# Expert loop: gather indices placed apart from the scatter's, sample's down products first and in another bank; attention: maxima moved ahead of a subtraction, one split step later

## What is computed

```python
def attend(q_blk):                       # 8 heads, query/key width 96, value width 64
    s = jnp.einsum('bqhd,bkhd->bhqk', q_blk, k)
    p = jax.nn.softmax(s, axis=-1)
    return jnp.einsum('bhqk,bkhd->bqhd', p, v)

def ec_moe(x, w_router, w_gate, w_up, w_down):     # 16 experts choose their tokens
    cap = max(1, EC_CAPACITY * N // N_EXPERTS)     # 256 of the prompt, 32 of the sample
    aff = jax.nn.softmax((xt @ w_router).astype(jnp.float32), axis=-1)
    gates, idx = lax.top_k(aff.T, cap)
    xs = xt[idx]
    h = jax.nn.silu(einsum(xs, w_gate)) * einsum(xs, w_up)     # 1024 -> 512
    y = einsum(h, w_down) * gates[..., None]                   # 512 -> 1024
    out = jnp.zeros((N, D), x.dtype).at[idx.reshape(-1)].add(y.reshape(-1, D))
```

## Time and profile before

| | us |
|---|---|
| median of 3 runs (lowest, highest) | 3238.51 (3237.43, 3239.25) |
| the profiled execution, its own time | 3233.96 |
| its span in the profile | 3232.1 |
| PE busy in the span | 2797.7 (87%) |
| DVE, ACT, POOL busy | 1780.7, 1564.5, 1089.2 |

### The profile page before, as it was taken

The page is one execution under the profiler, slowest core; times in us unless marked ns, Lnnn a source line. Parts: engine busy times, 40 slices in busy tenths (PEclk is TensorE's granted clock), DMA queues, the critical chain, the costliest instruction groups (busy, mean ns, idle before and its releaser), DMA issues. The chain is left out here.

```text
span 3232.1 us, 42082 instructions
## 1 busy us (share of the span) xinstructions
PE 2797.7 (87%) x15335; PEld 1523.0 (47%) x15335; DVE 1780.7 (55%) x2604; ACT 1564.5 (48%) x2488; POOL 1089.2 (34%) x969
## 2 busy tenths in 40 slices
PE   7999999959999999968976896999910899999998
PEld 4555555525555555522322232444400665566655
DVE  3344444448888888755567553333279444544443
ACT  3333333329999999955426441222240444444440
POOL 1111111127888888852036100121120232332321
PEclk9999999969999999989988997999955999999999
DMA  5112222224211111058975896443340556566562
GB/s 149 47 54 80 63 81 82 75 76 164 93 34 34 34 34 34 8 211 331 302 247 228 309 317 204 128 130 117 96 176 0 169 179 204 182 206 211 179 190 41
DMA packets 246139, 444.32 MB, mean 137 GB/s; under 512 B 55022, under 2 KB 136046, under 8 KB 244272
## 3 DMA queue, kind: packets, MB, share of 16 engines
q1 hardware_dynamic: 188608, 355.42, 33.1%
q0 software_dynamic: 10752, 37.75, 5.3%
q10 hardware_dynamic: 46608, 48.92, 4.7%
HBM read 290.25 MB, written 151.73 MB: 137 GB/s over the span
## 5 line engine op out<-in xcount | busy, mean ns | idle before, releaser
L959 POOL TENSOR_TENSOR at_p<-at_pf,at_p 128x512 f16<-128x512 f32 x424 | 515.3, 1227 | 143.8 <-ACT at_p L1093 119.9
L1221 DVE TENSOR_REDUCE at_mxs<-at_pM 128x1 f32<-128x512 f32 x512 | 342.3, 684 | 83.3 <-PE at_pM L1120 74.7
L578 PE MATMUL pj_ps<-pj_xT,pj_wch 128*128 128x512 f32 (+1 forms) x960 | 381.0, 550 | 0.8 <-issue 0.8
L1092 ACT ACTIVATE at_pf<-at_pS,at_scale 128x512 f32<-128x512 f32 x520 | 358.3, 689 | 40.5 <-PE at_pS L1145 40.4
L1093 ACT ACTIVATE at_p<-at_pS,at_scale 128x512 f16<-128x512 f32 x520 | 355.3, 683 | 0.0
L1164 PEld LDWEIGHTS at_pO<-at_vv,at_p 128*128 128x128 f16 x4160 | 234.0, 97 | 143.8 <-POOL at_p L959 34.6
L1164 PE MATMUL at_pO<-at_vv,at_p 128*128 128x129 f16 x4160 | 268.0, 207 | 10.2 <-POOL at_p L959 8.3
L578 PEld LDWEIGHTS pj_ps<-pj_xT,pj_wch 128*128 128x128 f32 x960 | 179.2, 190 | 167.9 <-issue 162.6
L1973 PE MATMUL mg_pU<-z,mg_yT 128*128 128x512 f32 x576 | 252.9, 597 | 0.2 <-ACT mg_yT L1882 0.2
L2540 PE MATMUL ex_pY<-mo_down,ex_hT 128*128 128x512 f32 x512 | 222.5, 592 | 0.7 <-issue 0.7
L1120 PE MATMUL at_pM<-at_k,at_q 96*128 96x512 f16 x512 | 190.1, 390 | 29.9 <-DVE at_q L1207 16.1
(11 more groups left out here) (279 smaller groups left out, 5360.4 us busy)
## 6 DMA issues: line engine op xcount, KB each, us to landing
sp_rows<-s_F SPq DMA_DIRECT2D x76, 768.0 KB, 6.9
s_F<-fs_a SPq DMA_DIRECT2D x72, 768.0 KB, 4.8
mo_raw<-in_w_gate SPq DMA_DIRECT2D x32, 1024.0 KB, 9.6
mo_raw<-in_w_up SPq DMA_DIRECT2D x32, 1024.0 KB, 10.1
mo_down<-in_w_down SPq DMA_DIRECT2D x16, 2048.0 KB, 11.1
s_G<-sp_gg ACTq DMA_DIRECT2D x72, 256.0 KB, 6.2
sp_tab<-tab_spec SPq DMA_DIRECT2D x76, 192.0 KB, 4.4
s_QK<-pj_R ACTq DMA_DIRECT2D x18, 768.0 KB, 4.4
```

The costliest lines, as they stand in the source:

```text
L578: last = pe.matmul(pU[n % 2][:, 0:width], wch[ch % 2][:, k, :], xT[:, k, t0:t0 + width], start=(k == 0), stop=(k == KD - 1))
L959: eng.tensor_tensor(p2[r][:, :], pf[:, r, :], p1[r][:, :], ALU.subtract).then_inc(own_done if n in own else others_done, 1)
L1092: act.activation(pf[:, n % 4, :], pS[n % 2][:, 0:QB], ACT.Exp, scale=scale[:, 0:1])
L1221: dve.tensor_reduce(mxs[:, j // NC, j % NC:j % NC + 1], pM[j % 2][:, :], AX.X, ALU.max).then_inc(pM_free, 1)
```

## The change

In the experts, `place` is cut in two. `place_gather(e + 1)` copies the gather's indices alone, at the start of the step, with no wait, and signals a semaphore of its own, `listed_g`, on which the gather now waits. `place(e)` copies the scatter's indices and the gates of the expert in hand, after `leave_x(e + 1)`, behind the wait for the scatters of expert e - 2. The order of the down products, their evictions and scatters is now sample, prompt tile 0, prompt tile 1 (DOWN_ORDER). The sample's products go into pU[1], one bank wide, in four groups of partitions, and not into pY; PE waits for its evictions before the next expert's second up product writes pU[1].

In attention, at the steps with a `move` (n % 16 = 7) DVE issues the `move` first and `rest` after it; at all other steps the order is as before. The twelfth split piece of heads 1 on is made at step 38, not 33 (it is the low part of one quarter of q, L1210).

```diff
--- before.py
+++ after.py
@@ -867,7 +867,7 @@
-    split_at = [1, 9, 11, 12, 14, 15, 17, 25, 27, 28, 30, 33, 41, 43, 44, 46]
+    split_at = [1, 9, 11, 12, 14, 15, 17, 25, 27, 28, 30, 38, 41, 43, 44, 46]
     first_split_at = [3, 6, 9, 11, 12]
     second_split_at = [22, 25, 27, 28, 30, 31, 33, 41, 43, 44, 46, 47, 49, 50, 52, 57]
     v_split_at = [5 + 14 * m for m in range(V_SPLITS)]
@@ -1275,11 +1275,16 @@
             def head(h, b):
                 for n in range(NS):
-                    rest_ahead(dve, own, h, n)
-                    for m in leads_in(h, n):
-                        ahead = leading(h, b, m)
+                    blocks = [leading(h, b, m) for m in leads_in(h, n)]
+                    moved = any(ahead and ahead[3] == last_in(ahead[0]) for ahead in blocks)
+                    if not moved:
+                        rest_ahead(dve, own, h, n)
+                    for ahead in blocks:
                         if ahead:
                             lead(*ahead)
+                    if moved:
+                        rest_ahead(dve, own, h, n)
                     if n % KT in range(norm_at, norm_at + 3):
                         part = (n % KT - norm_at,)
                         if n >= KT:
@@ -2058,6 +2063,8 @@
 PARTS = P // CAPS[1]
+DOWN_ORDER = (2, 0, 1)
 W_PARTS = 4
@@ -2380,7 +2387,7 @@
         part = sb("part", [CAPS[1], 512])
         wts, ticks = sem("wts"), sem("ticks")
         d_in = weights["d_in"]
-        placed = sem("placed")
+        listed_g, placed = sem("listed_g"), sem("placed")
         gathered = [sem(f"gathered{b}") for b in range(2)]
         x_low, multiplied, backed = sem("x_low"), sem("multiplied"), sem("backed")
         x_turned, xT_ready, gate_made, up_made = sem("x_turned"), sem("xT_ready"), sem("gate_made"), sem("up_made")
@@ -2432,7 +2439,7 @@
                 pool.tensor_tensor(mark[:, 1:2], mark[:, 0:1], mark[:, 0:1], ALU.add).then_inc(ticks, 1)
             def gather(e, b):
-                pool.wait_ge(placed, 3 * e + 3)
+                pool.wait_ge(listed_g, e + 1)
                 if not early(e):
                     pool.wait_ge(x_turned, TURNS * (e - 1))
                 tick((NC + 1) * e - NC if not isinstance(e, int) or e else 0)
@@ -2447,9 +2454,10 @@
                     gather(e + 1, 1 - b)
                 if not (isinstance(e, int) and e == 0):
                     pool.wait_ge(scattered, 16 * NC * e)
-                for c, (g, _, n) in enumerate(SLOT_TILES):
-                    pool.wait_ge(y_ready, 2 * NC * e + 2 * c + 2)
-                    tick((NC + 1) * e + 1 + min(more, 1) + c)
+                for i, c in enumerate(DOWN_ORDER):
+                    g, _, n = SLOT_TILES[c]
+                    pool.wait_ge(y_ready, 2 * NC * e + 2 * i + 2)
+                    tick((NC + 1) * e + 1 + min(more, 1) + i)
                     out = io[("y_prompt", "y_sample")[g]][0]
                     pool.indirect_dma_start(out=out, out_offset=bass.IndirectOffsetOnAxis(ap=now_s[b][0:n, c:c + 1], axis=0),
                                             in_=ys[b][c][0:n, :], in_offset=None, compute_op=ALU.add).then_inc(scattered, 16)
@@ -2521,6 +2529,8 @@
                     for g, (out, done, free) in enumerate(((pG, gate_made, silued), (pU, up_made, h_ready))):
                         if not (isinstance(e, int) and e == 0 and f < 2):
                             pe.wait_ge(free, FT * e + f - 1)
+                        if f == 1 and g and not (isinstance(e, int) and e == 0):
+                            pe.wait_ge(y_ready, 2 * NC * (e - 1) + 2)
                         if f == 0:
                             pe.wait_ge(weights["lo_made"], W_PARTS * e + 2 * g + 2)
                         for k in range(KD):
@@ -2532,25 +2542,26 @@
                     turn(e + 1, 1 - b)
                 pe.wait_ge(d_in[b], 8 * e - 8 * b + 16)
                 pe.wait_ge(h_ready, FT * e + FT)
+                at, n = starts[2], CAPS[1]
+                for r in range(2):
+                    for j in range(4):
+                        f, h = 2 * (j // 2) + r, j % 2
+                        last = pe.matmul(pU[1][n * j:n * j + n, :], hT[:, f, at:at + n],
+                                         wd[b][:, f, h * 512:(h + 1) * 512], start=(r == 0), stop=(r == 1))
+                        if r and j >= 2:
+                            last.then_inc(y_made, 1)
                 for c, (_, _, n) in enumerate(SLOT_TILES[:2]):
                     for h in range(2):
-                        if not (isinstance(e, int) and e == 0 and c == 0):
-                            pe.wait_ge(y_ready, 2 * NC * e + 2 * c + h - 1)
+                        if c:
+                            pe.wait_ge(y_ready, 2 * NC * e + 3 + h)
+                        elif not (isinstance(e, int) and e == 0):
+                            pe.wait_ge(y_ready, 2 * NC * e - 1 + h)
                         for f in range(FT):
                             last = pe.matmul(pY[0:n, h * 512:(h + 1) * 512], hT[:, f, starts[c]:starts[c] + n],
                                              wd[b][:, f, h * 512:(h + 1) * 512], start=(f == 0), stop=(f == FT - 1))
                         last.then_inc(y_made, 1)
-                pe.wait_ge(y_ready, 2 * NC * e + 4)
-                at, n = starts[2], CAPS[1]
-                for r in range(2):
-                    for j in range(4):
-                        f, h = 2 * (j // 2) + r, j % 2
-                        last = pe.matmul(pY[n * j:n * j + n, h * 512:(h + 1) * 512], hT[:, f, at:at + n],
-                                         wd[b][:, f, h * 512:(h + 1) * 512], start=(r == 0), stop=(r == 1))
-                        if r and j >= 2:
-                            last.then_inc(y_made, 1)
                 if more == 2:
                     pe.wait_ge(x_low, TURNS * e + 2 * TURNS)
                     add_squares(pe, weights, pN, e + 2)
@@ -2560,18 +2571,18 @@
         @block.vector
         def _(dve):
+            def place_gather(e, b):
+                dve.tensor_copy(now_g[b][:, :], chosen["gather"][:, :, bass.ds(e, 1)].rearrange("p c e -> p (c e)")
+                                ).then_inc(listed_g, 1)
             def place(e, b):
                 if not early(e):
                     dve.wait_ge(scattered, 16 * NC * (e - 1))
-                for dst, name in ((now_g, "gather"), (now_s, "scatter"), (now_w, "gate")):
-                    for_c = dst[b][:, :]
-                    if name == "gate":
-                        dve.tensor_copy(dst[b][:, 0:2], chosen[name][:, 0:2, bass.ds(e, 1)].rearrange("p c e -> p (c e)"))
-                        dve.tensor_copy(dst[b][0:CAPS[1], 2:3], chosen[name][0:CAPS[1], 2, bass.ds(e, 1)]).then_inc(placed, 1)
-                    else:
-                        dve.tensor_copy(for_c, chosen[name][:, :, bass.ds(e, 1)].rearrange("p c e -> p (c e)")).then_inc(placed, 1)
+                dve.tensor_copy(now_s[b][:, :], chosen["scatter"][:, :, bass.ds(e, 1)].rearrange("p c e -> p (c e)")
+                                ).then_inc(placed, 1)
+                gates = chosen["gate"]
+                dve.tensor_copy(now_w[b][:, 0:2], gates[:, 0:2, bass.ds(e, 1)].rearrange("p c e -> p (c e)"))
+                dve.tensor_copy(now_w[b][0:CAPS[1], 2:3], gates[0:CAPS[1], 2, bass.ds(e, 1)]).then_inc(placed, 1)
             def leave_x(e):
                 for m in range(TURNS):
@@ -2592,7 +2603,7 @@
             def step(e, b, more):
                 if more:
-                    place(e + 1, 1 - b)
+                    place_gather(e + 1, 1 - b)
                 for f in range(FT):
                     dve.wait_ge(silued, FT * e + f + 1)
                     dve.wait_ge(up_made, FT * e + f + 1)
@@ -2607,27 +2618,26 @@
                             make_lo(dve, weights, e + 1, 1 - b, i)
                 if more:
                     leave_x(e + 1)
-                if not early(e):
-                    dve.wait_ge(scattered, 16 * NC * (e - 1))
-                for c, (_, _, n) in enumerate(SLOT_TILES):
-                    if c == 0:
-                        dve.wait_ge(placed, 3 * e + 3)
+                place(e, b)
+                dve.wait_ge(placed, 2 * e + 2)
+                for i, c in enumerate(DOWN_ORDER):
+                    n = SLOT_TILES[c][2]
                     for h in range(2):
                         half = slice(h * 512, (h + 1) * 512)
-                        dve.wait_ge(y_made, 2 * NC * e + 2 * c + h + 1)
+                        dve.wait_ge(y_made, 2 * NC * e + 2 * i + h + 1)
                         if c == 2:
                             if h or not (isinstance(e, int) and e == 0):
-                                dve.wait_ge(y_ready, 2 * NC * e + 2 * c + h)
-                            dve.tensor_scalar(part[0:n, :], pY[n * h:n * h + n, half], now_w[b][0:n, c:c + 1], None, ALU.mult
+                                dve.wait_ge(y_ready, 2 * NC * e + h)
```

(5 more changed lines are left out.)

## The result

The changed kernel takes 3180.47 us (median of 4 runs, 3176.58 to 3183.51), the kernel before 3238.88 us in the runs beside it. The ratio is 0.9822 (95% interval 0.981 to 0.9835), a gain of 58.4 us. The forecast was 3193.5 and its range ended at 3187: the direction and the mechanism came out, the size did not. The profiled execution took 3178.97 us against 3233.96, 55.0 less.

What follows compares the result with a forecast made beforehand. PE sets an expert's length, so only its waits count, for late gathers and the sample's down products. Experts 39.6 plus attention 6 make 45.6, rounded to 45; 3238.5 - 45 = 3193.5 us, range 3187 to 3209.

Steps and rivals of the forecast that it cites:

- the length of the old expert loop: Experts: all 15 intervals between last prompt evictions, 659.37 us before; 621.0 without waits, so 38.4 us gained.
- attention's 6 us: Attention: `move` first ends PE's lost time ahead of maxima products; 6 us taken, bounds 0 and 6.9.
- Rival 4: Experts: gather lands so late that the kernel is slower; at t = 28, 55 us of waits, 3248; chance 0.02.
- Is the gather in time?: Experts: rows land 18 us after PE's down products end, PE wants them at 23.8; slack 5.8 us.
- the last starts 5.58 us later: Experts: last gather issued 5.58 us after the first, from t = 4.6 to about 10.2.
- Rival 3: Experts: gather late after all, behind all four loads; 1.5 us for 13 experts, 20 us, 3213; chance 0.06.
- The wait for pY: Experts: the sample's down products' wait for the last prompt tile's eviction goes; 0.84 us, 16 times, 13.5 us.
- the switch of shape: Experts: PE going from 128-column transposes to 32-column products costs zero to 0.84 us an expert; zero taken.
- rival 2: Experts: PE's change from 128-column transposes to 32-column products no longer hidden; up to 13.4 us, 3207 at most; chance 0.07.
- Rival 5: Experts: the wait only moves, as `place(e)` still stands behind `scattered`; nothing won, about 3232; chance 0.01.
- The tail: After the experts' last eviction: 11.9 us instead of 14.8, saving 2.9 us; the new order costs 1.9.
- cost nothing: Attention: split piece at step 38 fits DVE's 1.08 us of waiting; otherwise up to 4.8 us lost in 7 heads.

Runs made afterwards that it cites:

- the control: The kernel before, with no edit, submitted as if it were a change: 3238.09 us, ratio 0.9991.
- the two of the delayed gather: Changed kernel, each loop gather also waiting for the second or first hT of the expert in hand: 3262.15 us (second), 3180.17 us (first).

## Why the prediction was wrong

Two terms had the wrong size: the length of the old expert loop, 659.37 us, taken from a single execution, and attention's 6 us, for which 6.9 was held to be the upper bound. The mechanisms of both came out as described.

**The loop: right in every term, read from one execution that was not typical.** The waits that were to go went, and an interval is 41.41 us against the 41.48 worked out; all of them are 619.8 us against 621.0. The step that failed is the other end of the difference, the 659.37 us of before. Five profiles have the experts as before (the two of the kernel before, and the three in which only attention was edited): their stages of experts are 728.5 (the one that I read), 732.4, 734.6, 737.4 and 738.0 us. Mine was the shortest. In the control all 15 intervals sum to 667.1, 7.7 more than in mine: 2.6 of longer waits and three falls of the clock at 1.7. So two things vary. The gather's landing: its waits in the loop are 23.2 us in mine and 25.1 to 26 in the others. And the clock: mine is the only one of the five without a fall, the others have one to three, at 1.7 us each. With the middle one, 734.6, against 690.0 the experts give back 45 us, where I had 39.6. An average over executions can't be read from one. The prediction knew that the median of before was 4.5 us above the profiled execution, and added these 4.5 to the forecast as if after would have them too; the five profiles put a good part of such a difference into the loop that goes. The range reached 6.5 us below the forecast for all of it, against 15.5 above. The fault is thus in the range as well as in the term. One more piece of the stage had the wrong size without showing in the sum: from the end of the choice to expert 0's last prompt eviction after took 57.9 us and before 54.2, so 3.6 were lost where 1.9 - 0.2 = 1.7 were worked out (54.1 to 56.1 in the five profiles, 56.2 to 57.9 in six with the new experts). What the other 1.9 us are is open.

**The clock as a term was missing.** I wrote "at a granted clock of 1.00" and took from it that the waits cost their own length. A wait of 2 us here costs 2 us and, some of the time, 1.7 more; one of 3 to 5 us in 11 of 14 cases. Rival 4 has the same omission: at 55 us of waits I had the time at 3248, and with such waits it came to 3262, although after itself was 13 us faster than forecast. The half clock is 22 us of it.

**Is the gather in time? Right, with a slack that was too small.** I had 5.8 us, the runs show about 9. The step that failed is "the last starts 5.58 us later": in before the gathers were issued beside the low halves of the weights, in after nearly all of them are issued before a low half runs. Only the third meets one, in 6 of 13 experts, and then takes 2.8 to 2.9 us. The grouped rows of POOL, after and then before, in 500 us of the loop (in all, mean ns):

```profile
L2448 POOL DMA_INDIRECT ex_xs<-s_XN,ex_now_g x36 | 46.7, 1296 | 11.0 <-issue 11.0
```

```profile
L2441 POOL DMA_INDIRECT ex_xs<-s_XN,ex_now_g x33 | 78.5, 2379 | 12.4 <-issue 12.4
```

A duration was carried from one neighbourhood to another. Here it erred on the safe side. Rival 3 falls with it.

**The wait for pY and the switch of shape: right.** 0.84 us each was to go, 0.91 went, and rival 2 is refuted. That the sample's evictions do not hold up the prompt's holds too: the interval is PE's own work. Rival 5 falls as well: in the experts of after DVE has no wait for a scatter.

**The order alone: not worked out.** The prediction summed the order's 13.4 us as if independent of the placing. It is worth 14 us behind it and 6 without it (10 by the one profile's stage against 734.6), for the loop then takes back part of what PE saves: the waits for the gathers grow. Since both were made, the sum is unharmed.

**The tail: right.** From the last eviction to the end there are 3177.2 - 3165.01 = 12.2 us, where 11.9 were worked out and 14.8 were before. The last scatter of after:

```profile
3166.20 1.57 POOL L2462 DMA_INDIRECT y_prompt<-ex_ys,ex_now_s  x1 [0.16 <-issue]
```

SP's first load of gate weights came 9.5 us after its load of down weights (2720.26 against 2710.80), as forecast (9.4).

**Attention: the mechanism right, 4 of 10 us missing.** The step that failed is "I take 6 of the 6.9 us", with 6.9 as its upper bound. In all 30 places the lost time is gone. The timeline of after at one of them:

```profile
1052.01 0.27 PE L1128 MATMUL at_pM<-at_eye,at_mx 128*4 128x128 f32 x1
...
1052.32 0.28 DVE L1238 TENSOR_SCALAR at_nmx<-at_pM 4x128 f16<-4x128 f32 x1 [0.36 <-PE at_pM L1128]
...
1052.53 1.18 DVE L959 TENSOR_TENSOR at_p<-at_pf,at_p 128x512 f16<-128x512 f32 x1
...
1053.22 0.53 PE L1164 MATMUL at_pO<-at_vv,at_p 128*128 128x129 f16 x8 [0.28 <-POOL at_p L959]
...
1053.58 0.59 PE L1120 MATMUL at_pM<-at_k,at_q 96*128 96x512 f16 x2
```

`move` starts 0.3 us after the transpose and the maxima product follows the values product by its 0.36 us, as predicted; in the earlier trace rows it was 0.79. But the stage is 10 to 12 us shorter (707.7 to 710.2 in five kernels with the old order, with the piece moved alone left out; 697.5 to 699.9 with the new). By the table above 10 of these are the change, 8.5 behind the first head and 1.5 in it; the other 2 are the moment at which the clock rose. What I had as ACT's to take back went the other way. Once in most heads PE waited 0.36 us for POOL's `rest` in a later block, in the kernel before as here:

```profile
1079.89 0.52 PE L1164 MATMUL at_pO<-at_vv,at_p 128*128 128x129 f16 x8 [0.36 <-POOL at_p L959]
```

I had booked this as POOL's own and left it in. It is gone in every kernel with `move` first: PE's waits for POOL fall from 8.3 us in 23 to 6.4 in 18. A head takes 1052.01 to 1132.99, 81.0 us, not 82.25. Why POOL comes in time then is argued, not shown: after the changed block all three engines run earlier, and POOL, which in before made five subtractions without a pause up to and past this place (6.40 us from 1075.73), makes three, waits 0.45 us for ACT, and makes two.

**The split piece: "cost nothing" holds only with the other edit.** Alone it costs about 5 us by the times and 3.5 by the stage; 4.8 was what I had written as its bad end. The step that failed is the 1.08 us of idle time, read from a kernel in which the piece was at step 33. With `move` first it costs nothing that shows, and brings nothing.

**What the sum leaves open.** 45 from the experts and 10 from attention are 55 of the 58.4. Of the 13 us by which the forecast fell short, 5 are thus the old loop's length, 4 attention, and the rest is open. The part between them, which no edit touches, took 1112.6 to 1115.2 us in the five profiles with all of the change (the two of the delayed gather among them), and 1113.1 to 1119.7 in the others, the control being at 1113.1. Of the 6.3 us between the two profiles that I compared first, most is therefore scatter; whether the last 3 us belong to the change is not settled.

## What to carry to other kernels

When a loop of waits is to be removed, work out the length without it, which one execution tells well (41.48 against 41.41), but take the length with it from several executions: a loop that hangs on DMA landings varies, and an engine's gaps may cost clock besides their own length. If an index for a read shares a copy step with an index for a write that must wait, place the two apart, and do this before any reordering behind it: the order alone gave 6 us, behind the placing 14. And where two engines exchange one short result in a fixed order of long operations, the consumer of the short result goes first.

## What the runs showed of the hardware

- **A gap of 2 us can be followed by half clock on TensorE.** In five profiles of the old loop, with gaps of 1.7 to 2.6 us (and one of 0.5), 0 to 3 of 12 were followed by about 3.4 us at the 1.2 GHz level, which cost 1.7 us. With gaps of 3.2 to 4.7 us it was 11 of 14, and four of these falls were 6.8 us long. In the loop of after, without gaps, there was none.
- **POOL's small instruction can wait for DVE.** The marking instruction of 128 x 1 takes 0.18 us in after, and 2.06 us where it met DVE's low halves (4.61 us for the two from 2753.74, so the first ended near 2756.05, and the mark at 2756.13). A gather's issue takes 0.95 to 1.05 us when no low half is running at its start and, in before, 1.8 to 3.2 when one is. The Trainium skill, SBUF — State Buffer, section SBUF: two separate sides, says that DVE and GpSimd share one pair of ports as an exclusive lock, which a DVE operation with two SBUF inputs takes against a GpSimd operation that reads SBUF; the mark, ending with the first low half, agrees.
- **The size of an accumulating scatter shows in its landing.** From issue to DVE's release 32 rows took 6.8 us (2740.96 to 2747.80 in the kernel before) and 128 rows 9.4 us (2733.78 to 2743.19 in the kernel with the order alone). Within after the 16 scatters of 32 rows landed in 3.5 to 3.7 us and the 32 of 128 rows in 5.9 to 10.4. The neighbouring DMA traffic is not the same in these cases, so the rows are not the only difference.
